# Silu in one ScalarE operation, a different VectorE order at the second phase of the way down, and the last two pairs of the last tile in two pieces

## The chip, the core and the metric

The kernel runs on one core of one Trainium2 chip. The metric is the time of one execution on the device in microseconds (us), as the median of several runs. Engines: TensorE (PE) multiplies matrices, VectorE (DVE) and ScalarE (ACT) work on tiles, GpSimd (POOL) does small things here, SyncE (SP) issues all large transfers.

## The reference

One layer of an encoder block on x of 512 tokens by 1024 channels, all in float32, then a final RMSNorm. The change touches the second half of the layer, a SwiGLU:

```
h = rms_norm(x, ffn_norm)                      # 512 x 1024
a, b = split(h @ w_gate_up, 2)                 # w_gate_up 1024 x 5632, a and b 512 x 2816
x = x + (silu(a) * b) @ w_down                 # silu(a) = a * sigmoid(a); w_down 2816 x 1024
return rms_norm(x, final_norm)
```

The first half (RMSNorm, one input projection of 6664 columns, forgetting attention, pooling, short convolution, gates, output projection) is the same in both kernels.

## The kernel before

**Arithmetic.** Every float32 product is made of three matmuls on split operands. A weight tile w is cast by ScalarE into a high part (`whi`), VectorE subtracts it from w to get the low part (`wlo`), and TensorE adds high*high, high*low and low*high. So every weight tile goes over SyncE (load into `raw`), ScalarE (`split_hi`, `parts_hi`, which raise `w_hi`), VectorE (`split_lo`, L1283; `parts_lo`, L1598, which raise `w_lo`) and TensorE. `raw`, `whi` and `wlo` are rings; SyncE's next load into a slot waits for `w_lo` of the unit that held it.

**Gate and up** (stages `ffn_first`, `ffn`, `ffn_last`). For each of 22 blocks of 128 hidden units TensorE makes two banks of 128x512, the gate and the up half. VectorE scales each by the row's 1/rms (`gate_rows`, L1625, `up_rows`, L1630), ScalarE computes the sigmoid of the gate into `SG`, and VectorE multiplies gate by sigmoid (L1617) and that by up (L1619). Two blocks form a pair; for a pair VectorE then makes the differences and sums that the way down uses (`hid_sum`), and splits them (`hid_low`).

**The way down** (product with `w_down`) is one level of a Strassen-like scheme with 7 products instead of 8, over R = 11 pairs, in four phases of TensorE. Phase 1 makes two products for every pair, 12 matmuls of 128x512 a pair, into banks `AB` and `DB_`. Phase 2 makes three, 18 matmuls a pair, into `FB_`, `DB_` and `AB`. Phase 3 makes one into `EB`, phase 4 one onto `FB_`. The weights of a product are blocks of `w_down` or sums of them, which VectorE also makes (`first_sum`, L1607; `second_sums`, L1716 and L1717; `third_sum`). Nothing plans this order at run time: it is written out by hand, one queue for each engine, and all waits are on semaphores. An engine that waits holds up all that stands behind it in its queue.

**Where phase 1 passes to phase 2.** TensorE's first pair of phase 2 (r = 0) takes in turn `FB_` (needs `w_lo` of the first two parts), `AB` (needs the third part, and `added` of 1 and 2: VectorE has added what the two `AB` banks held to the output x2), and `DB_` (needs `added` of 3 and 4). The next pair (r = 1) begins with `FB_` and the first two parts of its weights. VectorE's order for r = 0 is: two parts of pair 0 (one instruction, L1598), `second_sums(1)` (two), the third part of pair 0, `added` 1 and 2, `added` 3 and 4 (four instructions of L1741), `second_lo(8)` (L1681, the low part of hidden sums that TensorE needs for pair 8). Then r = 1 begins with two parts of pair 1.

**The end.** In phase 4 TensorE finishes `FB_[0]` for all pairs, then adds pairs 5 to 9 into `FB_[1]`, and puts the last pair (r = 10) of the last tile of tokens into two other banks in two pieces of 256 columns. VectorE adds `FB_[1]` to x2 (L1879), then each piece (`x2_piece`, L1833), scales tile 2 for output (`right_out(2)`, L1853), adds up the squares of the first piece that ScalarE made (L1888), makes those of the second piece (L1891) and the variance (L1840). GpSimd raises it to -0.5 (L577), ScalarE (`left_out`, L1244) and VectorE (`right_out`) scale the last tile, and SyncE writes it (L519), in the order left, right of tile 2, then left, right of each piece. ScalarE squares the first piece (L1237) and scales the left half of tile 2 after it.

Of the kernel before, what the change touches and what calls it, by code (L numbers as in the profile page):

```python
# [64 lines left out]

    "vector_step": dict(norm=19, front=23, pair=13, mix=2, ffn_first=7, ffn=15, ffn_last=8,
                        down=4),
# [34 lines left out]
def hybrid_block(nc, x, attn_norm, w_in, b_forget, b_gate, w_proj_attn, pool_w, pool_scale,  # L102
# [26 lines left out]
    with ExitStack() as ctx:  # L129
# [153 lines left out]
        def wk(slot, n=S, rows=slice(0, P)):  # L283
            return work[rows, slot * S:slot * S + n]
# [28 lines left out]
        ROWS4 = [(r,) for r in range(4)] + [(r, r + 1) for r in range(4, R - 1, 2)] + [(R - 1,)]  # L313
        LATE = 5
        ROWS3 = [(0,)] + [(r, r + 1) for r in range(1, R, 2)]
# [269 lines left out]
        def _(pe):  # L585
# [312 lines left out]
            mm.then_inc(full[FB_[0]], 1)  # L898
            for r in range(LATE, R - 1):
                mm = times(FB_[1], hid(r, A22 - 2), hid(r, A22), U_4 + r, 1, False, r == R - 2, True)  # L900
            mm.then_inc(full[FB_[1]], 1)
            pe.wait_ge(added, 14)
            for piece, b in zip(PIECES[TB - 1], LAST_BANKS):
                times(b, hid(R - 1, A22 - 2), hid(R - 1, A22), U_4 + R - 1, 1, True, True,
                      piece=piece).then_inc(full[b], 1)

# [4 lines left out]
        def _(act):  # L911
# [226 lines left out]
            def hidden(stage, i, j):  # L1138

                wait_free(act, (2 * j + 2) % 6, stage, i, j // 3 + 1)  # L1140
                tile(wk(SG), wk(A1), ACT.Sigmoid)
                split_hi(stage, i, 2 * j + 3)
                if stage != "ffn_first" and j % 2 == 0:
                    r = i * 3 + j // 2 if stage == "ffn" else R - 2 + j // 2
                    act.wait_ge(hid_sums, r + 1)
                    nc.scalar.copy(hid(r, S1_ + 2, 2), hid_32(r, S1_, 2)).then_inc(hid_hi, 1)  # L1146
                split_hi(stage, i, 2 * j + 4)
# [5 lines left out]
            tile(stat[:, 12:16], stat[:, 8:12], ACT.Exp, scale=-0.5)  # L1153
            nc.scalar.preload_act_table(ACT.Sigmoid)
            wait_full(act, 6, "ffn_first", 0, 1)
# [7 lines left out]
            wait_free(act, 0, "ffn_first", 0, 1)  # L1163
            tile(wk(SG), wk(A1), ACT.Sigmoid)
            split_hi("ffn_first", 0, 3)
# [5 lines left out]
            wait_free(act, 4, "ffn_last", 0, 1)  # L1171
            tile(wk(SG), wk(A1), ACT.Sigmoid)
            split_hi("ffn_last", 0, 5)
            second_hi(0)
            down_hi(0)
            wait_free(act, 0, "ffn_last", 0, 1)
            tile(wk(SG), wk(A1), ACT.Sigmoid)
            second_hi(1)
# [82 lines left out]
        def _(dve):  # L1261
# [348 lines left out]
            def gate_times_up(stage, i, j, r, odd):  # L1610

                a = (2 * j + 2) % 6 if stage != "ffn_first" else 0
                k = j // 3 + 1
                wait_free(dve, a, stage, i, k)
                dve.wait_ge(scalar_tile, count("scalar_tile", stage, i,
                                               j + 1 if stage != "ffn_first" else 3))
                step(nc.vector.tensor_tensor(wk(HD_), wk(A1), wk(SG), ALU.mult))  # L1617
                wait_free(dve, a + 1, stage, i, k)
                step(nc.vector.tensor_tensor(hid_32(r, A12 if odd else A11, 2), wk(HD_), wk(B1),  # L1619
                                             ALU.mult))  # L1620
# [144 lines left out]
            for r in range(R):  # L1765
                u, s = U_2 + 3 * r, (R + r) % SLOTS
                parts_lo(u, raw[:, s, 0:2 * HALF], 2)
                if r + 1 < R:
                    second_sums(r + 1)
                parts_lo(u + 2, chain(r))  # L1770
                if r == 0:
                    for m in range(2):
                        bank_done(AB[m], 1, U_2 - 2)
                        add_bank(AB[m], m, 1, ALU.add)
                    for m in range(2):
                        bank_done(DB_[m], 1, U_2 - 1)
                        add_bank(DB_[m], 2 + m, 0, ALU.subtract)
                if r < 3:
                    second_lo(R - 3 + r)
                if r >= 3:  # L1780
                    third_lo(r - 3)

            third_low(0)
            third_lo(R - 3)
            third_sum(0)
# [80 lines left out]
            for t in range(2):  # L1866
# [12 lines left out]
            step(nc.vector.tensor_tensor(tok(big_x, t, 1), banks[FB_[1]][:], tok(big_x, t, 1),  # L1879
                                         ALU.add))  # L1880
            x2_piece(t, 0)
            x2_piece(t, 1)
            right_out(2)
            lo, hi = PIECES[t][1]
            x2 = tok(big_x, t, 1)[:, lo:hi]
            dve.wait_ge(x2_square, t + 1)
            part = stat[:, SS_SUM:SS_SUM + 1]
            step(nc.vector.scalar_tensor_tensor(out=part, in0=square_sum(t), scalar=1.0 / D,  # L1888
                                                in1=left_part(t), op0=ALU.mult, op1=ALU.add))
            dve.wait_ge(x2_done, TB + 1)  # L1890
            step(nc.vector.scalar_tensor_tensor(  # L1891
                out=wk(HD_, hi - lo), in0=x2, scalar=1.0, in1=x2, op0=ALU.mult,
                op1=ALU.mult, accum_out=square_sum(TB)))
            variance(t, square_sum(TB), part)
# [28 lines left out]
```

## Time and profile before

| | |
|---|---|
| runs (us) | 806.82, 808.43, 2974.62; median 808.43 |
| profiled execution (us) | 808.46 |
| its span, first to last instruction (us) | 806.4 |
| TensorE busy | 787.4 us, 98% |
| VectorE busy | 505.2 us, 63% |
| ScalarE busy | 324.0 us, 40% |
| GpSimd busy | 21.0 us, 3% |
| granted TensorE clock, mean | 0.997 |

In the rows below a start is in us from the start of the span, the number behind it is the length in us, and brackets give the engine's idle time before the instruction and what ended it. Matmuls overlap, so the distance of their starts counts, not their length. The same holds for VectorE: an instruction of 0.69 us that waits for nothing lets the next one start after about 0.60 us.

### The profile page before, as it was taken

What the parts mean: (1) busy time and instruction counts of PE and PEld (TensorE: products, weight loads), DVE (VectorE), ACT (ScalarE), POOL (GpSimd) and SP (SyncE); (2) the same over time, 40 slices, a digit from 0 to 9 for tenths busy, and PEclk for the clock granted to TensorE, in tenths of its full rate; (3) what the DMA queues carried; (4) which work ended last, traced back from release to release, by engine and by line L of the source; (5) the groups of instructions that cost most, each with busy time, mean ns of one, the idle gap of its engine ahead of it and who ended that gap; (6) DMA issues with size and microseconds to landing.
All of it is one profiled execution on the core that took longest, in us unless ns stands there. A gap on an engine that the chain in (4) does not pass through costs nothing.

```text
span 806.4 us, 10953 instructions
## 1 busy us (share of the span) xinstructions
PE 787.4 (98%) x3568; PEld 652.7 (81%) x3568; DVE 505.2 (63%) x763; ACT 324.0 (40%) x520; POOL 21.0 (3%) x43
## 2 busy tenths in 40 slices
PE   5999999999999999999999999999999999999996
PEld 4878888888888888888888888888888888877885
DVE  7878686868634333443333465555555556799996
ACT  7265555555422222232223532222222222565554
POOL 4011010100000000000000000000000000000001
PEclk9999999999999999999999999999999999999998
DMA  7423232323243333334233233333333332353522
GB/s 223 124 78 92 56 100 55 101 54 102 56 110 96 104 104 97 85 91 117 81 102 99 59 105 94 89 104 104 104 92 90 104 104 88 123 170 118 164 85 104
DMA packets 128670, 81.18 MB, mean 101 GB/s; under 512 B 5420, under 2 KB 118116, under 8 KB 128644
## 3 DMA queue, kind: packets, MB, share of 16 engines
q1 hardware_dynamic: 128132, 80.79, 34.1%
q8 instruction: 14, 0.23, 0.1%
q0 software_dynamic: 512, 0.07, 0.1%
q14 instruction: 12, 0.10, 0.0%
HBM read 78.67 MB, written 2.10 MB: 100 GB/s over the span
## 4 chain that ended last, share of the span: by engine, by line
PE 92%; DVE 5%; DMA 1%; issue 1%; ACT 0%; SPq 0%; POOLq 0%; POOL 0%; ACTq 0%; DVEq 0%
PE bank L600 24%; PE bank L604 24%; PE bank L602 24%; PE bank L859 3%; PE bank L861 3%; PE bank L860 3%; PE bank L781 2%; PE bank L777 2%; PE bank L779 2%; PE bank L714 1%; DVE wlo L1598 1%; PE bank L631 1%; DVE operands L1681 1%; PE bank L694 1%; PE bank L739 1%
## 5 line engine op out<-in xcount | busy, mean ns | idle before, releaser
L600 PE MATMUL bank<-operands,whi 128*128 128x512 f32 x864 | 338.1, 391 | 1.0 <-DVE operands L1292 1.0
L604 PE MATMUL bank<-operands,wlo 128*128 128x512 f32 x864 | 336.4, 389 | 0.0
L602 PE MATMUL bank<-operands,whi 128*128 128x512 f32 x864 | 336.2, 389 | 0.0
L1283 DVE TENSOR_TENSOR wlo<-raw,whi 128x1024 fp32r<-128x1024 f32 x116 | 142.0, 1225 | 140.2 <-ACT whi L918 137.4
L600 PEld LDWEIGHTS bank<-operands,whi 128*128 128x128 f32 x864 | 162.2, 188 | 34.7 <-issue 1.4
L604 PEld LDWEIGHTS bank<-operands,wlo 128*128 128x128 f32 x864 | 162.2, 188 | 34.3
L602 PEld LDWEIGHTS bank<-operands,whi 128*128 128x128 f32 x864 | 162.2, 188 | 33.4 <-issue 0.2
L918 ACT CAST whi<-raw 128x1024 fp32r<-128x1024 f32 x116 | 121.1, 1045 | 70.4 <-PE bank L604 47.9
L924 ACT ACTIVATE work<-work 128x512 f32<-128x512 f32 (+1 forms) x24 | 15.2, 632 | 82.9 <-DVE work L1625 80.8
L1065 ACT ACTIVATE work<-bank,vecs 128x512 f32<-128x512 f32 x24 | 16.6, 690 | 78.0 <-PE bank L604 78.0
L1522 DVE TENSOR_TENSOR work<-bank,work 128x512 f32<-128x512 f32 x24 | 15.8, 688 | 41.1 <-PE bank L604 29.6
L861 PE MATMUL bank<-whi,operands 128*128 128x512 f32 x96 | 37.4, 390 | 0.0
L921 ACT ACTIVATE operands<-work 128x512 f32 (+2 forms) x24 | 15.2, 632 | 54.5 <-DVE work L1539 27.5
L859 PE MATMUL bank<-whi,operands 128*128 128x512 f32 x90 | 35.3, 392 | 0.0
L860 PE MATMUL bank<-wlo,operands 128*128 128x512 f32 x90 | 35.0, 389 | 0.0
L1146 ACT CAST operands<-tiles (+1 forms) x10 | 6.2, 622 | 62.4 <-DVE tiles L1636 62.4
L1630 DVE TENSOR_TENSOR work<-bank,big_y 128x512 f32<-128x512 f32 x22 | 15.2, 691 | 24.1 <-PE bank L604 24.0
L1625 DVE TENSOR_TENSOR work<-bank,big_y 128x512 f32<-128x512 f32 x22 | 15.1, 688 | 22.6 <-PE bank L604 17.6
L1022 ACT ACTIVATE big_y<-big_y,stat 128x128 f32<-128x128 f32 (+3 forms) x32 | 17.6, 552 | 22.1 <-DVE stat L1454 21.6
L1290 DVE TENSOR_TENSOR operands<-work,operands 128x512 f32 (+2 forms) x24 | 16.6, 690 | 14.4 <-ACT operands L921 13.4
L777 PE MATMUL bank<-whi,operands 128*128 128x512 f32 x64 | 25.0, 390 | 0.0
L781 PE MATMUL bank<-whi,operands 128*128 128x512 f32 x64 | 24.9, 389 | 0.0
(213 smaller groups left out, 842.3 us busy)
## 6 DMA issues: line engine op xcount, KB each, us to landing
raw<-in_w_in_dram SPq DMA_DIRECT2D x106, 256.0 KB, 3.2
raw<-in_w_gate_up_dram SPq DMA_DIRECT2D x88, 256.0 KB, 3.1
raw<-in_w_down_dram SPq DMA_DIRECT2D x55, 256.0 KB, 2.9
raw<-in_w_out_dram SPq DMA_DIRECT2D x16, 256.0 KB, 3.0
big_x<-in_x_dram SPq DMA_DIRECT2D x4, 512.0 KB, 3.8
raw<-in_w_proj_attn_dram SPq DMA_DIRECT2D x8, 256.0 KB, 2.8
raw<-in_w_proj_pool_dram SPq DMA_DIRECT2D x8, 256.0 KB, 3.1
raw<-in_w_proj_conv_dram SPq DMA_DIRECT2D x8, 256.0 KB, 3.0
```

The source lines that it names most:

```text
L600: nc.tensor.matmul(banks[b][:, 0:width], whi[:, s, w], op(hi + k * S), start=a, stop=False)
L602: nc.tensor.matmul(banks[b][:, 0:width], whi[:, s, w], op(lo + k * S), start=False, stop=False)
L604: mm = nc.tensor.matmul(banks[b][:, 0:width], wlo[:, s, w], op(hi + k * S), start=False, stop=z)
L777: nc.tensor.matmul(to, op(hi + at, P), whi[:, s, w], start=a, stop=False)
L781: mm = nc.tensor.matmul(to, op(lo + at, P), whi[:, s, w], start=False, stop=z)
L859: nc.tensor.matmul(to, h, wh, start=first, stop=False, skip_group_check=onto)
L860: nc.tensor.matmul(to, h, wl, start=False, stop=False, skip_group_check=onto)
L861: return nc.tensor.matmul(to, l, wh, start=False, stop=last, skip_group_check=onto)
L918: nc.scalar.copy(whi[:, s, :], raw[:, s, :]).then_inc(w_hi, 1)
L1022: e = nc.scalar.activation(lg, lg, ACT.Exp, bias=stat[:, 16 + at:17 + at], accum_out=stat[:, 24 + at:25 + at])
L1065: nc.scalar.activation(wk(GA + br), banks[b][:], ACT.Sigmoid, bias=vecs[:, bass.ds(i * 2 + (V_GATE + br * DB + mm), 1)]).then_inc(free[b], 1)
L1283: nc.vector.tensor_tensor(wlo[:, s, :], raw[:, s, :], whi[:, s, :].bitcast(F32), ALU.subtract).then_inc(w_lo, 1)
```

## The change

The sigmoid becomes `Silu` with the table preloaded for it, and VectorE's L1617 goes, so that the product with up (L1619) reads `SG` directly; its wait for the gate bank goes too, the one for the up bank stays. In phase 2 `second_sums(1)` moves behind `added` 1 and 2 and ahead of `added` 3 and 4, each `second_lo` moves from r to r+1 (first from r = 0 to r = 1), and each `third_lo` by one as well, so that one of them comes after the first part of phase 3. In phase 4 pairs 9 and 10 both go in two pieces of 256 columns, so that `FB_[1]` is full one pair earlier. VectorE scales tile 2 for output before it adds the pieces, and makes the second piece's squares before it takes in those of the first. No transfer is added or removed, and SyncE's and GpSimd's code is the same.

```diff
--- before.py
+++ after.py
@@ -63,7 +63,7 @@
     "row_max": dict(pair=2), "exp_done": dict(pair=2), "probs": dict(pair=2),
     "v_lo_part": dict(pair=2),
 
-    "vector_step": dict(norm=19, front=23, pair=13, mix=2, ffn_first=7, ffn=15, ffn_last=8,
+    "vector_step": dict(norm=19, front=23, pair=13, mix=2, ffn_first=6, ffn=9, ffn_last=5,
                         down=4),
 }
 
@@ -311,7 +311,7 @@
         AB, DB_, FB_, EB = (2, 3), (6, 7), (4, 5), (0, 1)
         N1 = 0
         ROWS4 = [(r,) for r in range(4)] + [(r, r + 1) for r in range(4, R - 1, 2)] + [(R - 1,)]
-        LATE = 5
+        LATE, LAST = 5, R - 2
         ROWS3 = [(0,)] + [(r, r + 1) for r in range(1, R, 2)]
 
 
@@ -896,13 +896,16 @@
                 pe.wait_ge(w_lo, U_4 + r + 1)
                 mm = times(FB_[0], hid(r, A22 - 2), hid(r, A22), U_4 + r, 0, False, r == R - 1, True)
             mm.then_inc(full[FB_[0]], 1)
-            for r in range(LATE, R - 1):
-                mm = times(FB_[1], hid(r, A22 - 2), hid(r, A22), U_4 + r, 1, False, r == R - 2, True)
+            for r in range(LATE, LAST):
+                mm = times(FB_[1], hid(r, A22 - 2), hid(r, A22), U_4 + r, 1, False, r == LAST - 1,
+                           True)
             mm.then_inc(full[FB_[1]], 1)
             pe.wait_ge(added, 14)
             for piece, b in zip(PIECES[TB - 1], LAST_BANKS):
-                times(b, hid(R - 1, A22 - 2), hid(R - 1, A22), U_4 + R - 1, 1, True, True,
-                      piece=piece).then_inc(full[b], 1)
+                for r in range(LAST, R):
+                    mm = times(b, hid(r, A22 - 2), hid(r, A22), U_4 + r, 1, r == LAST, r == R - 1,
+                               piece=piece)
+                mm.then_inc(full[b], 1)
 
 
 
@@ -1138,7 +1141,7 @@
             def hidden(stage, i, j):
 
                 wait_free(act, (2 * j + 2) % 6, stage, i, j // 3 + 1)
-                tile(wk(SG), wk(A1), ACT.Sigmoid)
+                tile(wk(SG), wk(A1), ACT.Silu)
                 split_hi(stage, i, 2 * j + 3)
                 if stage != "ffn_first" and j % 2 == 0:
                     r = i * 3 + j // 2 if stage == "ffn" else R - 2 + j // 2
@@ -1151,7 +1154,7 @@
             tile(stat[:, 8:12], stat[:, 4:8], ACT.Ln)
             act.wait_ge(scalar_tile, count("scalar_tile", "ffn_first", 0, 1))
             tile(stat[:, 12:16], stat[:, 8:12], ACT.Exp, scale=-0.5)
-            nc.scalar.preload_act_table(ACT.Sigmoid)
+            nc.scalar.preload_act_table(ACT.Silu)
             wait_full(act, 6, "ffn_first", 0, 1)
             nc.scalar.copy(RSTD, banks[6][:]).then_inc(free[6], 1)
             def second_hi(r):
@@ -1161,7 +1164,7 @@
                 nc.scalar.copy(high2(r, S4_, 3), hid_32(r, S4_, 3)).then_inc(hid2_hi, 1)
 
             wait_free(act, 0, "ffn_first", 0, 1)
-            tile(wk(SG), wk(A1), ACT.Sigmoid)
+            tile(wk(SG), wk(A1), ACT.Silu)
             split_hi("ffn_first", 0, 3)
             split_hi("ffn_first", 0, 4)
             with act.Fori(0, 3) as i:
@@ -1169,12 +1172,12 @@
                     hidden("ffn", i, j)
             hidden("ffn_last", 0, 0)
             wait_free(act, 4, "ffn_last", 0, 1)
-            tile(wk(SG), wk(A1), ACT.Sigmoid)
+            tile(wk(SG), wk(A1), ACT.Silu)
             split_hi("ffn_last", 0, 5)
             second_hi(0)
             down_hi(0)
             wait_free(act, 0, "ffn_last", 0, 1)
-            tile(wk(SG), wk(A1), ACT.Sigmoid)
+            tile(wk(SG), wk(A1), ACT.Silu)
             second_hi(1)
             down_hi(1)
             act.wait_ge(hid_sums, R)
@@ -1611,12 +1614,10 @@
 
                 a = (2 * j + 2) % 6 if stage != "ffn_first" else 0
                 k = j // 3 + 1
-                wait_free(dve, a, stage, i, k)
                 dve.wait_ge(scalar_tile, count("scalar_tile", stage, i,
                                                j + 1 if stage != "ffn_first" else 3))
-                step(nc.vector.tensor_tensor(wk(HD_), wk(A1), wk(SG), ALU.mult))
                 wait_free(dve, a + 1, stage, i, k)
-                step(nc.vector.tensor_tensor(hid_32(r, A12 if odd else A11, 2), wk(HD_), wk(B1),
+                step(nc.vector.tensor_tensor(hid_32(r, A12 if odd else A11, 2), wk(SG), wk(B1),
                                              ALU.mult))
 
             def gate_rows(stage, i, j):
@@ -1765,22 +1766,24 @@
             for r in range(R):
                 u, s = U_2 + 3 * r, (R + r) % SLOTS
                 parts_lo(u, raw[:, s, 0:2 * HALF], 2)
-                if r + 1 < R:
+                if 1 <= r < R - 1:
                     second_sums(r + 1)
                 parts_lo(u + 2, chain(r))
                 if r == 0:
                     for m in range(2):
                         bank_done(AB[m], 1, U_2 - 2)
                         add_bank(AB[m], m, 1, ALU.add)
+                    second_sums(1)
                     for m in range(2):
                         bank_done(DB_[m], 1, U_2 - 1)
                         add_bank(DB_[m], 2 + m, 0, ALU.subtract)
-                if r < 3:
-                    second_lo(R - 3 + r)
-                if r >= 3:
-                    third_lo(r - 3)
+                if 1 <= r < 4:
+                    second_lo(R - 4 + r)
+                if r >= 4:
+                    third_lo(r - 4)
 
             third_low(0)
+            third_lo(R - 4)
             third_lo(R - 3)
             third_sum(0)
             third_low(1)
@@ -1878,19 +1881,19 @@
             dve.wait_ge(added, 14)
             step(nc.vector.tensor_tensor(tok(big_x, t, 1), banks[FB_[1]][:], tok(big_x, t, 1),
                                          ALU.add))
+            right_out(2)
             x2_piece(t, 0)
             x2_piece(t, 1)
-            right_out(2)
             lo, hi = PIECES[t][1]
             x2 = tok(big_x, t, 1)[:, lo:hi]
+            dve.wait_ge(x2_done, TB + 1)
+            step(nc.vector.scalar_tensor_tensor(
+                out=wk(HD_, hi - lo), in0=x2, scalar=1.0, in1=x2, op0=ALU.mult,
+                op1=ALU.mult, accum_out=square_sum(TB)))
             dve.wait_ge(x2_square, t + 1)
             part = stat[:, SS_SUM:SS_SUM + 1]
             step(nc.vector.scalar_tensor_tensor(out=part, in0=square_sum(t), scalar=1.0 / D,
                                                 in1=left_part(t), op0=ALU.mult, op1=ALU.add))
-            dve.wait_ge(x2_done, TB + 1)
-            step(nc.vector.scalar_tensor_tensor(
-                out=wk(HD_, hi - lo), in0=x2, scalar=1.0, in1=x2, op0=ALU.mult,
-                op1=ALU.mult, accum_out=square_sum(TB)))
             variance(t, square_sum(TB), part)
             right_out(t)
             leave()
```

## Rows read from the trace of the kernel before

**Rows 1.** Busy time of each engine in two stretches: us, instructions in brackets

```profile
400.00:600.00 200.00, 200.00 (x898) 165.69 (x897) 106.71 (x143) 62.28 (x87) 0.00 (x0) 1.00 0.32 95
...
720.00:740.00 20.00, 17.95 (x77) 13.97 (x77) 20.00 (x28) 9.93 (x15) 0.00 (x0) 1.00 0.38 125
```

**Rows 2.** The gate's multiplication, grouped by line, from 400 us to the end

```profile
L1617 DVE TENSOR_TENSOR work<-work 128x512 f32<-128x512 f32 x22 | 15.0, 683 | 0.0
```

**Rows 3.** VectorE in order of time, 691 to 727 us: start, length, idle before

```profile
691.19 0.69 DVE L1630 TENSOR_TENSOR work<-bank,big_y 128x512 f32<-128x512 f32 x1 [0.65 <-PE bank L604]
691.80 0.68 DVE L1617 TENSOR_TENSOR work<-work 128x512 f32<-128x512 f32 x1
692.52 0.69 DVE L1619 TENSOR_TENSOR last_tile<-work 128x512 f32<-128x512 f32 x1
...
704.66 0.69 DVE L1607 TENSOR_TENSOR early<-raw 128x512 f32<-128x512 f32 x1 [2.65 <-DMA raw<-in_w_down_dram]
...
720.72 1.22 DVE L1598 TENSOR_TENSOR wlo<-raw,whi 128x1024 fp32r<-128x1024 f32 x1
...
723.66 2.47 DVE L1741 TENSOR_TENSOR big_x<-big_x,bank 128x512 f32<-128x512 f32 x4
726.05 0.95 DVE L1681 TENSOR_TENSOR operands<-tiles,operands 128x768 fp32r<-128x768 f32 x1
726.92 1.22 DVE L1598 TENSOR_TENSOR operands<-raw,operands 128x1024 fp32r<-128x1024 f32 x1
```

**Rows 4.** TensorE in order of time: first matmuls of the way down, then the transition

```profile
690.99 0.39 PE L859 MATMUL bank<-whi,operands 128*128 128x512 f32 x1
...
722.03 0.47 PE L859 MATMUL bank<-whi,high 128*128 128x512 f32 x1 [0.41 <-issue]
...
724.48 0.47 PE L859 MATMUL bank<-operands,high 128*128 128x512 f32 x1 [0.82 <-DVE big_x L1741]
...
728.28 0.47 PE L859 MATMUL bank<-operands,high 128*128 128x512 f32 x1 [0.81 <-DVE operands L1598]
```

**Rows 5.** The seventh load of the way down: SyncE's issues, then time to landing

```profile
L487 SPq DMA_DIRECT2D raw<-in_w_down_dram x2: 327/863/1399, 699.6 to 700.0; - x2
...
DMA to landing us min/median/max: 3.0/3.8/4.7
```

**Rows 6.** ScalarE in order of time: casts before and after a table load

```profile
694.50 0.61 ACT L1128 CAST whi<-raw 128x512 fp32r<-128x512 f32 x1
695.02 0.61 ACT L1128 CAST whi<-flat 128x512 fp32r<-128x512 f32 x1
695.65 1.28 ACT L1190 ACT_TABLE_LOAD   x1
696.95 0.62 ACT L1128 CAST operands<-raw 128x512 fp32r<-128x512 f32 x1
```

**Rows 7.** All engines in order of time at the end, 797 to 802 us

```profile
797.41 0.55 POOL L577 TENSOR_TENSOR stat<-stat 128x1 f32<-128x1 f32 x1 [2.60 <-DVE stat L1840]
...
798.22 0.39 PE L861 MATMUL bank<-whi,operands 128*128 128x512 f32 x1
...
798.45 0.28 PE L859 MATMUL bank<-whi,last_tile 128*128 128x256 f32 x1
...
798.65 0.69 DVE L1879 TENSOR_TENSOR big_x<-bank,big_x 128x512 f32<-128x512 f32 x1 [1.31 <-PE bank L861]
...
799.37 0.76 DVE L1833 TENSOR_TENSOR big_x<-bank,big_x 128x256 f32<-128x256 f32 x2
...
800.04 0.74 DVE L1853 SCALAR_TENSOR_TENSOR tiles<-big_x,stat,work 128x512 f32<-128x512 f32 x1
...
800.70 0.15 DVE L1888 SCALAR_TENSOR_TENSOR stat<-stat 128x1 f32<-128x1 f32 x1
800.89 0.43 DVE L1891 SCALAR_TENSOR_TENSOR work<-big_x 128x256 f32<-128x256 f32 x1
...
801.60 0.55 POOL L577 TENSOR_TENSOR stat<-stat 128x1 f32<-128x1 f32 x1 [3.64 <-DVE stat L1840]
```

## The prediction

> **What bounds the kernel now.** I read the busy time by stretch first, for which engine is full where. In the long gate-and-up stage TensorE is busy for all of 200.00 us and VectorE for 106.71; in the 20 us around the passage to the second phase it is the other way round, VectorE 20.00 and TensorE 17.95 [rows 1]. So VectorE work taken away before that passage is worth nothing to the end, and in it each microsecond may count. Then VectorE and TensorE in order of time. From 728.28 us to the row at 798.22 TensorE issues 308 further matmuls of 512 columns (180 of phase 2's last ten pairs, 66 of phase 3, 63 of phase 4, less the first): 69.94 us, or 0.227 each, without a pause [rows 4, 7]. By that pace the way down's first matmul at 690.99, with 132 matmuls in phase 1 and 18 in pair 0 of phase 2 behind it, would reach pair 1 at 690.99 + 150 x 0.227 = 725.04 us. It does at 728.28. **3.24 us** are lost there, some in phase 1, the rest in the waits of [rows 4], and that is all that the passage can give back.
>
> Who holds it up is VectorE: pair 1 starts 1.36 us after VectorE starts on its weights (726.92 to 728.28), and VectorE works without a gap from 704.66 to there [rows 3, 4]. Its last idle time, 2.65 us before 704.66, ends with the seventh load of the way down [rows 3]. SyncE issued that load when VectorE had finished weights two operations earlier, so it too hangs on VectorE; one of its two issues took 1.40 us where the other took 0.33, and one half landed after 4.7 us, the other after 3.0 [rows 5]. The last stretch, after TensorE, is one chain: VectorE adds the pieces, squares, makes the variance, GpSimd takes the power at 801.60, and 4.8 us of scaling and writing follow to 806.4 [rows 7].
>
> **The change, part by part.**
>
> *Silu.* It removes 22 multiplications of 683 ns, 15.0 us of VectorE [rows 2]. 21 lie where TensorE has no pause, cover enough even if ScalarE's Silu took twice the sigmoid's time, so I count them as nothing. The last one stands at 691.80, ahead of the way down. It started 0.61 us after the scaling of the up half (691.19) and needed no wait for it; the next product started 0.72 later, at 692.52, after a wait [rows 3]. Without it that product has to wait for the scaling itself, to 691.19 + 0.72 = 691.91. The gain is 692.52 - 691.91 = **0.61 us**, not 0.72. Everything behind it up to the seventh load follows a chain of VectorE, ScalarE and SyncE without slack that I can find, so I take the load, and the start at 704.66, to move with it. Bounds: 0 if the landing time does not follow, and if the 1.40 us issue falls back to the other's 0.33, 1.07 more [rows 5]. I take 0.61 as VectorE's code changes and SyncE's does not. A Silu that cost ScalarE more would be late at nobody here: between its tile and 691.19 VectorE waits 0.65 us for TensorE [rows 3].
>
> *The order at the passage.* `second_lo(8)`, 726.05 to 726.92, was ahead of pair 1's weights and now is behind them: **0.87 us** [rows 3]. Nobody needs it before pair 8. With the two moves the weights of pair 1 start at 726.92 - 0.61 - 0.87 = 725.44 and TensorE's pair 1 at 725.44 + 1.36 = 726.80. The other half of this edit, `second_sums(1)` between the two pairs of additions, moves no work across pair 1; it makes the `AB` additions earlier and leaves the `DB_` additions last. Does one of them bind? Four additions take 2.39 (723.66 to 726.05), 0.60 each, so the first for `DB_` starts at 725.44 - 1.20 = 724.24. TensorE started 0.82 after such an addition did (723.66 to 724.48), so at 725.06 [rows 3, 4]. Six matmuls, 1.36, make it 726.42, before 726.80. They bind nothing but eat what the early `AB` wins. The pauses then are 0.47 ahead of pair 0 (its weights at 720.11, 1.31 later at 721.42, against 690.99 + 132 x 0.227 = 720.95), 0.92 ahead of `DB_` (721.42 + 12 x 0.227 = 724.14), 0.38 ahead of pair 1: 1.77 of the 3.24 remain. Late next is VectorE again. After that it needs for a pair the two-part operation (1.22 long, 1.13 to the next, as 0.69 gives 0.60), three short ones and a `second_lo`: 1.13 + 3 x 0.60 + 0.87 = 3.80 us [rows 3], against 18 x 0.227 = 4.09 of TensorE, so no new wait builds up. ScalarE's cast for pair 1 waits for the first of the moved sums: from 724.24 - 1.20 = 723.04 to 723.73. Two parts take about 2 x 0.52 = 1.04 (estimated from [rows 6]), so it is there at 724.8, 0.6 before 725.44. The moved low parts of phase 3 lie under TensorE's 4.09 us a pair: nothing. Passage: 0.61 + 0.87 = **1.48 us**. SyncE's loads of phase 2 wait for weights that come earlier or at the same place in the queue, so no load is put off.
>
> *The last two pairs in pieces.* Three matmuls of 512 columns become six of 256. The only rows of such pieces are the six from 798.45; the first three take the time to a pitch near 0.118 against half of 0.227, 0.03 us more in all [rows 7]. `FB_[1]` is full three matmuls earlier, so its addition goes from 798.65 to 797.97; VectorE was idle for 1.31 before it [rows 7]. The copy-out of tile 2 comes next, at 797.97 + 0.72 = 798.69 (GpSimd's power for it is done at 797.96), and takes 0.66 (800.04 to 800.70). So the pieces are added from 799.35, as before (799.37), and TensorE's last piece ends at about the old time, 799.35, before the second one needs it. Two additions take 0.67 (799.37 to 800.04) and the wait for the second about 0.1: the squares start at 800.12. From there to GpSimd was 0.71, and now the small sum of 0.19 (800.70 to 800.89) lies between [rows 7]: 800.12 + 0.71 + 0.19 = 801.02, say 801.05 with the 0.03. Gain: 801.60 - 801.05 = **0.55 us**. Nothing of the pieces themselves; the copy-out in the idle time makes it. Bounds: 0 if the writes behind it cannot start sooner, 0.66 if the whole copy-out goes.
>
> Sum, against the profiled execution: 808.46 - 1.48 - 0.55 = **806.4 us**. The median of the runs shown is 808.43, so the same holds for it.
>
> **Rivals.**
>
> *The landing does not follow.* The seventh load comes when it did; Silu gives nothing, and 808.46 - 0.87 - 0.55 = 807.0. For it: one issue of 1.40 us in [rows 5] that no operation of VectorE explains. Against: the load is issued by VectorE's progress.
>
> *The landing gets shorter.* The 1.40 us issue was an accident, and 1.07 us more come off: 805.4. The floor is 808.46 - 3.24 - 0.55 = 804.7.
>
> *The writes bind.* SyncE writes tile 2's left half first, which ScalarE makes no sooner than before, and the last four writes then share the way with it. The tail gives 0: 807.0.
>
> *Table loads, and slower than before.* If Silu's table did not serve the casts as well, ScalarE would change tables before every Silu and again behind it. A load put the next cast 1.93 us behind the last (695.02 to 696.95) where casts follow after 0.52 (694.50 to 695.02), so 1.41 a switch [rows 6]. In the gate-and-up stage that is hidden, as TensorE has no pause and ScalarE is busy for 62.28 of 200 us [rows 1]. At the last Silu, two switches put off weights that stand ahead of 691.19 in VectorE's queue by 2.82 us; 0.65 of idle time there absorbs a part [rows 3]. The total is 2 x 1.41 - 0.65 - 0.61 - 0.87 - 0.55 = +0.14: 808.6. It turns from gain to loss at 1.34 us a switch. Against it: the sigmoid lives with the same casts, and the load in [rows 6] stands where the code asks for one. The Trainium skill's page "ScalarE: Activation LUTs", section "What ACT_TABLE_LOAD costs", gives 1.28 us and a drain of 1.38, 2.66 us for a switch; at that price this rival would be 811.1, but the row shows the 1.28 and no such drain. The same page's section "Table sets: the hidden batching unit" says that cheap functions such as copy are in every set, which speaks against the rival; no row here has a Silu in it.
>
> *It does not do what it says.* Silu's last gain and the order's are both taken up by a wait that I don't see (ScalarE's cast for pair 1 is the closest): 808.46 - 0.55 = 807.9.
>
> **Numbers.** Forecast as summed 0.5; landing fixed 0.13; landing shorter 0.15; writes bind 0.08; a hidden wait 0.1; table loads 0.04. The range goes from the floor, 804.7, to 808.3, which takes in all but the last case and also that two runs of the kernel before differ by 1.6 us. Two per cent, about what a measurement of this kernel can tell from no change, is 16 us; no case comes near it: within 2% 0.98, 0.01 on either side.
>
> **What would show it.** Right: no multiplication at L1617 and as many table loads as before; the idle time before the way down's seventh load ends about 0.6 us earlier; `DB_` of pair 0 waits about 0.9 us, pair 1 starts about 1.5 us earlier against the way down's first matmul; the last power starts 2.0 us earlier than 801.60, and 4.8 us follow. Wrong: a pause of TensorE later than pair 1, a table load between Silu and a cast, VectorE waiting for ScalarE's cast at pair 1, or more than 5 us behind the last power.

## The result: 2.0 us faster, ratio 0.9975

| | before | changed |
|---|---|---|
| median of 13 runs each (us) | 807.39 | 804.84 |
| ratio, 95% interval | | 0.9975 [0.9967, 0.9983] |
| profiled execution, its span (us) | 808.46, 806.4 | 806.28, 804.3 |

The ratio is 2.0 us of 808 (1.4 to 2.7); the medians alone are 2.55 apart. The one run of 2974.62 us among those before is left out of the ratio. Forecast were 806.4 against 808.46, so 2.03 us, and the range of 804.7 to 808.3 holds the 804.84 near its lower end. A second comparison in another series gave 0.9974 [0.9964, 0.9985]. The intervals are about 0.1% wide to each side, much finer than the two per cent of the forecast.

The two spans differ by 2.1 us, but they can't be set side by side as they are. From TensorE's first product of a weight tile on, the marks below compare them. The way down's first matmul came 1.45 us later in the changed kernel, because the transfers at the start took longer (the four of x took 4.5 us to land in the median, 3.8 before); the 675.0 us between are equal.

| mark (us) | before | changed | difference |
|---|---|---|---|
| first product of a weight tile | 15.96 | 17.38 | +1.42 |
| from there to the way down's first matmul | 675.03 | 675.06 | +0.03 |
| from there to pair 1 of phase 2 | 37.29 | 34.30 | -2.99 |
| from there to the last power on GpSimd | 73.32 | 72.72 | -0.60 |
| from there to the end | 4.8 | 4.8 | 0.0 |

The profile after, busy time of the engines in the stretches of [rows 1]:

```profile
400.00:600.00 200.00, 200.00 (x899) 165.70 (x898) 99.61 (x131) 62.61 (x86) 0.00 (x0) 1.00 0.32 94
...
720.00:740.00 20.00, 19.90 (x89) 16.08 (x88) 20.00 (x29) 10.55 (x15) 0.00 (x0) 1.00 0.41 132
```

VectorE has 7 us less to do in the long stage and no other engine is faster for it. In the passage VectorE is still full, but TensorE's pause has shrunk from 2.05 to 0.10 us.

All lines with a table load, from the groups by line (count, then busy us and mean ns), and the 22 gate functions, from the groups by line and shape behind 400 us:

```profile
L930 ACT ACT_TABLE_LOAD x1 | 1.3, 1283 | 0.7 <-PEq L1914 0.7
L1058 ACT ACT_TABLE_LOAD x1 | 1.3, 1283 | 0.0
L1152 ACT ACT_TABLE_LOAD x1 | 1.3, 1283 | 0.0
L1157 ACT ACT_TABLE_LOAD x1 | 1.3, 1283 | 0.0
L1193 ACT ACT_TABLE_LOAD x1 | 1.3, 1283 | 0.0
```

```profile
L927 ACT ACTIVATE work<-work 128x512 f32<-128x512 f32 x22 | 13.9, 632 | 80.2 <-DVE work L1626 80.2
```

Five loads, each where the code asks for one, as before; a Silu takes 632 ns, as the sigmoid did. The rival with table loads is dead. The Trainium skill's page "ScalarE: Activation LUTs", section "Table sets: the hidden batching unit", says that copy is in every set, and the trace agrees.

VectorE in order of time, the instructions that answer to [rows 3], and TensorE's that answer to [rows 4]:

```profile
692.64 0.69 DVE L1631 TENSOR_TENSOR work<-bank,big_y 128x512 f32<-128x512 f32 x1 [0.65 <-PE bank L604]
693.44 0.69 DVE L1620 TENSOR_TENSOR last_tile<-work 128x512 f32<-128x512 f32 x1
...
703.80 0.69 DVE L1610 TENSOR_TENSOR early<-raw 128x512 f32<-128x512 f32 x1 [0.98 <-DMA raw<-in_w_down_dram]
...
724.18 1.28 DVE L1742 TENSOR_TENSOR big_x<-big_x,bank 128x512 f32<-128x512 f32 x2
725.38 1.22 DVE L1601 TENSOR_TENSOR operands<-raw,operands 128x1024 fp32r<-128x1024 f32 x1
```

```profile
692.44 0.39 PE L859 MATMUL bank<-whi,operands 128*128 128x512 f32 x1
...
725.09 0.39 PE L859 MATMUL bank<-whi,high 128*128 128x512 f32 x1
...
726.74 0.47 PE L859 MATMUL bank<-operands,high 128*128 128x512 f32 x1
```

Against the way down's first matmul (690.99 before, 692.44 here) the sum on the seventh load moved from +13.67 to +11.36, by 2.31 us and not by 0.61. `DB_` starts at +32.65, its own pace (144 x 0.227 = 32.69), without the wait of 0.92 that was forecast. Pair 1 is at +34.30, 0.25 from that pace. The seventh load's issues and landings, to compare with [rows 5]:

```profile
L487 SPq DMA_DIRECT2D raw<-in_w_down_dram x2: 327/377/427, 700.5 to 700.9; - x2
...
DMA to landing us min/median/max: 2.5/2.7/2.9
```

No issue of 1.40 us and no landing of 4.7. This is the rival "the landing gets shorter": the gain ahead of pair 1 came out at 2.99 instead of 1.48. It was priced at 1.07 us, from the issues alone; the later half landed 1.8 us sooner after its issue began (2.9 against 4.7). And the end, to compare with [rows 7]:

```profile
796.18 0.28 PE L859 MATMUL bank<-whi,operands 128*128 128x256 f32 x1
...
796.38 0.69 DVE L1882 TENSOR_TENSOR big_x<-bank,big_x 128x512 f32<-128x512 f32 x1 [0.64 <-PE bank L861]
...
797.11 0.75 DVE L1856 SCALAR_TENSOR_TENSOR tiles<-big_x,stat,work 128x512 f32<-128x512 f32 x1
...
797.78 0.75 DVE L1836 TENSOR_TENSOR big_x<-bank,big_x 128x256 f32<-128x256 f32 x2
...
798.56 0.42 DVE L1890 SCALAR_TENSOR_TENSOR work<-big_x 128x256 f32<-128x256 f32 x1
...
799.03 0.16 DVE L1895 SCALAR_TENSOR_TENSOR stat<-stat 128x1 f32<-128x1 f32 x1
...
799.46 0.55 POOL L577 TENSOR_TENSOR stat<-stat 128x1 f32<-128x1 f32 x1 [3.09 <-DVE stat L1843]
```

VectorE's idle time ahead of the full bank fell from 1.31 to 0.64, the copy-out stands in what is now free, and the squares start 0.78 after the first piece's addition, where 1.52 were (799.37 to 800.89).

### The profile page after: what moved, and what is told of

Read it like the earlier page. It is cut to its first block, busy times and chain, and to the rows that moved or that the text cites. A ratio compares the mean times of both kernels' runs of the same rounds, so it can differ in the third digit from the quotient of the medians.

```text
span 804.3 us, 10900 instructions
## 1 busy us (share of the span) xinstructions
PE 786.6 (98%) x3571; PEld 653.7 (81%) x3571; DVE 491.9 (61%) x741; ACT 324.2 (40%) x520; POOL 20.5 (3%) x43
## 4 chain that ended last, share of the span: by engine, by line
PE 96%; DVE 1%; issue 1%; DMA 1%; ACT 0%; POOLq 0%; POOL 0%; ACTq 0%; SPq 0%; DVEq 0%
PE bank L600 24%; PE bank L602 24%; PE bank L604 24%; PE bank L859 4%; PE bank L861 4%; PE bank L860 4%; PE bank L777 2%; PE bank L779 2%; PE bank L781 2%; PE bank L714 1%; PE bank L694 1%; PE bank L739 1%; PE bank L692 1%; PE bank L737 1%; DMA big_x<-in_x_dram 1%
## 5 line engine op out<-in xcount | busy, mean ns | idle before, releaser
L1068 ACT ACTIVATE work<-bank,vecs 128x512 f32<-128x512 f32 x24 | 16.5, 689 | 78.0 <-PE bank L604 78.0
L1525 DVE TENSOR_TENSOR work<-bank,work 128x512 f32<-128x512 f32 x24 | 15.8, 688 | 41.2 <-PE bank L604 29.6
L861 PE MATMUL bank<-whi,operands 128*128 128x512 f32 (+1 forms) x97 | 37.5, 387 | 0.0
L860 PE MATMUL bank<-wlo,operands 128*128 128x512 f32 (+1 forms) x91 | 35.2, 387 | 0.0
L859 PE MATMUL bank<-whi,operands 128*128 128x512 f32 (+1 forms) x91 | 35.2, 387 | 0.0
L1293 DVE TENSOR_TENSOR operands<-work,operands 128x512 f32 (+2 forms) x24 | 16.5, 689 | 14.4 <-ACT operands L924 13.4
L777 PE MATMUL bank<-whi,operands 128*128 128x512 f32 x64 | 25.0, 390 | 0.0
L781 PE MATMUL bank<-whi,operands 128*128 128x512 f32 x64 | 24.9, 389 | 0.0
```

Of the source, the lines that this page charges most:

```text
L777: nc.tensor.matmul(to, op(hi + at, P), whi[:, s, w], start=a, stop=False)
L781: mm = nc.tensor.matmul(to, op(lo + at, P), whi[:, s, w], start=False, stop=z)
L859: nc.tensor.matmul(to, h, wh, start=first, stop=False, skip_group_check=onto)
L860: nc.tensor.matmul(to, h, wl, start=False, stop=False, skip_group_check=onto)
L861: return nc.tensor.matmul(to, l, wh, start=False, stop=last, skip_group_check=onto)
L1068: nc.scalar.activation(wk(GA + br), banks[b][:], ACT.Sigmoid, bias=vecs[:, bass.ds(i * 2 + (V_GATE + br * DB + mm), 1)]).then_inc(free[b], 1)
```

## The experiments

Open after this: why the landing differs, whether each part is worth what the sum says, and which part of the tail makes it. Twelve further kernels ran (two of them without an edit), each timed in five rounds and profiled once. All marks are in us: "seventh load" is VectorE's first sum on it and "pair 1" the first matmul of pair 1 in phase 2, both from the way down's first matmul; "tail" goes from pair 1 to the last power. "Behind" is the power to the end. The interval of a ratio is about 0.0009 wide to each side, 0.7 us, and the ratios of the three parts alone (e2, e3, e4) can't be told from 1. That can't size a part, so the marks do; each comes from one profiled execution of its kernel. Code cuts leave out the counts of VectorE's steps, which change with the edit.

| | seventh load | pair 1 | tail | behind | ratio |
|---|---|---|---|---|---|
| before, as first profiled | 13.67 | 37.29 | 73.32 | 4.8 | |
| changed, as first profiled | 11.36 | 34.30 | 72.72 | 4.8 | 0.9975 |
| e1 before again | 12.16 | 35.78 | 73.32 | 4.8 | 1.0010 |
| e2 Silu only | 11.36 | 35.08 | 73.30 | 4.8 | 0.9998 |
| e3 order only | 11.86 | 34.66 | 73.30 | 4.8 | 1.0001 |
| e4 tail only | 12.68 | 36.30 | 72.76 | 4.8 | 1.0000 |
| e5 changed again | 11.36 | 34.80 | 72.76 | 4.8 | 0.9974 |
| e6 product back in 21 blocks | 11.37 | 34.15 | 72.74 | 4.8 | 0.9975 |
| e7 product back in the last | 11.87 | 34.63 | 72.73 | 4.8 | 0.9977 |
| e8 pieces, VectorE as before | 11.43 | 34.31 | 72.98 | 4.8 | 0.9973 |
| e9 VectorE's tail, no pieces | 11.34 | 35.04 | 73.44 | 4.8 | 0.9986 |
| e10 before, low part moved | 12.01 | 37.29 | 73.30 | 4.8 | 1.0007 |
| e11 changed, low part moved | 11.70 | 35.65 | 72.71 | 4.8 | 0.9985 |
| e12 and small sum on ScalarE | 13.10 | 35.15 | 72.71 | 5.0 | 0.9987 |

**e1, the kernel before once more.** No edit.

> The kernel before, once more, against itself. Ratio 1.000 within 0.001. Marks, measured from the first matmul of the way down in each profile: VectorE's first sum on the seventh load at +13.67 us in the first profile, +11.36 with the change; first matmul of pair 1 of phase 2 at +37.29 and +34.30. Theory 1 (the 1.40 us issue of the seventh load and its late landing were an accident of one execution): this run shows issues of 0.33 to 0.43 us, the seventh load at about +12.0 (11.36 + 0.61) and pair 1 at about +35.8. Theory 2 (it belongs to the kernel before and its timing, and Silu took it away): again an issue over 1 us, +13.7 and +37.3.

The same code, 1.5 us earlier at the seventh load, and 23.62 us from there to pair 1 both times. The sum on the seventh load in e1, and its two issues:

```profile
703.17 0.69 DVE L1607 TENSOR_TENSOR early<-raw 128x512 f32<-128x512 f32 x1 [1.24 <-DMA raw<-in_w_down_dram]
```

```profile
L487 SPq DMA_DIRECT2D raw<-in_w_down_dram x2: 328/376/425, 699.6 to 700.0; - x2
...
DMA to landing us min/median/max: 2.5/2.9/3.2
```

Theory 1 holds: the late landing was luck of the execution, not of the code. Even so e1's sum is 0.3 us later than in e3, which has the same code up to there: both issue the load at the same mark, and its later half took 3.2 us to land in e1 and 2.9 in e3. The traces show one thing that differs between the two executions of the kernel before. In each of the 14 there is one transfer of 16 KB, of the kind that the profile calls "instruction", between +8 and +17 of the way down. The row of it in the kernel before from 699.3 to 699.6 us, at +8.5, and in e1 from 707.1 to 707.4, at +16.3 (queue, packets, MB, share):

```profile
q8 instruction: 1, 0.02, 30.1%
```

```profile
q8 instruction: 1, 0.02, 20.8%
```

At +8.5 it falls on the seventh load's issue, in the kernel before and in e4, and those two have late sums, 13.67 and 12.68. The third late one, 13.10 in e12, has it at +10.6, while half of that load was on its way. In the changed kernel it came at +15.5, beside the tenth load, where VectorE waited only 0.09 us. That the transfer causes the late landing is an inference from its place in these traces; no run moved it on purpose. The ratio of 1.0010 [1.0001, 1.0019] for equal code tells how far a ratio here is to be trusted: e2 to e4, taken in the same series, are 0.0012, 0.0009 and 0.0010 below it, 0.7 to 1.0 us each, with intervals as wide as that.

**e2, Silu only**, and **e7, the product put back in the last block** of the changed kernel (its result is not used; cut from the edit):

```diff
+                if stage == "ffn_last" and j == 2:
+                    step(nc.vector.tensor_tensor(wk(HD_), wk(A1), wk(SG), ALU.mult))
```

> Silu alone; order and tail as before. Theory 1: seventh load at +11.4 where its landing is normal, pair 1 0.61 us earlier than in the run of the kernel before of this job (if that one is at +35.8, here +35.2), time 0.6 us less, ratio 0.9992. Theory 2: landing 2.3 us earlier than the kernel before, pair 1 at +35.0 against +37.3, time 2.3 us less, ratio 0.997. Rival with table loads: more than 5 ACT_TABLE_LOAD in the trace and a ratio over 1.

> The changed kernel with that multiplication put back in the last block alone, 0.68 us of VectorE. Prediction's step: the seventh load and pair 1 of phase 2 come 0.61 us later than in the changed kernel with the same landing: VectorE's first sum on the seventh load at +12.0 (+11.4 without), but pair 1 at most 0.4 us later where TensorE had reached its own pace. Rival: no shift, the gain was the landing alone.

Where the landing is undisturbed the sum on the seventh load stands at 11.34 to 11.43 with Silu (the changed kernel, e2, e5, e6, e8, e9) and at 11.86 and 11.87 without its effect in the last block (e3, e7). So the last product is worth **0.50 us** there. SyncE's issue shows it free of the landing: the seventh load's starts at +8.06 or +8.07 in all eight executions with Silu's effect in the last block, and at +8.59 in all six without it, 0.53 us later. So the load follows VectorE, as the forecast assumed. The two issues in the changed kernel and in e7, whose first matmuls of the way down start at 692.44 and 690.77:

```profile
700.50 0.80 SPq L487 DMA_DIRECT2D raw<-in_w_down_dram  x2
```

```profile
699.36 0.80 SPq L487 DMA_DIRECT2D raw<-in_w_down_dram  x2
```

The scaling and the products in e7:

```profile
690.97 0.69 DVE L1633 TENSOR_TENSOR work<-bank,big_y 128x512 f32<-128x512 f32 x1 [0.64 <-PE bank L604]
691.57 0.68 DVE L1620 TENSOR_TENSOR work<-work 128x512 f32<-128x512 f32 x1
692.29 0.69 DVE L1622 TENSOR_TENSOR last_tile<-work 128x512 f32<-128x512 f32 x1
```

1.32 us from the scaling to the product with up. Without the middle one it is 0.80 (692.64 to 693.44 in the changed kernel), not the 0.72 of the forecast, and from the 1.33 between the two in the kernel before (691.19 to 692.52) that leaves the gain of 0.53. Why it is 0.80 is not shown. That the scaling reads a bank does not explain it: in an earlier stage of the changed kernel a sum that waits for a product which reads a bank starts 0.73 after it (406.25 to 406.98, L1525 to L1542). The product with up waits for ScalarE's `SG` as well, in the code.

**e6, the product put back in the other 21 blocks** (same lines with `not`).

> The changed kernel with the multiplication of gate and gate function put back on VectorE in the first 21 of 22 blocks (its result is not used). 14.3 us of VectorE more. Prediction's step: worth nothing, all marks and the time as in the changed kernel within 0.1 us, ratio as e5. Rival (VectorE's load counts in the long stage): TensorE's 675.0 us from its first weight product to the way down grow, or the ratio goes back towards 1.

14.3 us more of VectorE and nothing moved later: 675.02 us to the way down, seventh load at 11.37, pair 1 at 34.15. The part costed at nothing is worth nothing.

**e3, the order only.**

> The new order at the passage alone. Both theories: pair 1 0.87 us earlier than the kernel before with the same landing, and nothing before the passage changes: with a normal landing +34.9 (theory 1), with the late one +36.4 (theory 2). From pair 1 to the last power 73.3 us as before. Ratio 0.9989. If the additions into the DB banks bind, a wait of TensorE for VectorE's L1741 of about 0.9 us ahead of the DB matmuls.

From the seventh load to pair 1 it is 22.80 us instead of 23.62: **0.82** of the 0.87 forecast, with Silu away. The landing was a little sooner than the one of e1, so pair 1 came at 34.66.

**e4, the tail only; e8, pieces with VectorE's old order; e9, VectorE's new order without the pieces.** e8 takes the change's hunk on TensorE alone, e9 the one on VectorE's end alone, both with Silu and the order at the passage.

> Pieces of the last two pairs and VectorE's new order at the end alone. From pair 1 to the last power 72.7 us instead of 73.3, 4.8 us behind it, pair 1 where the kernel before has it. Ratio 0.9993. If the writes bind: 5.4 us behind the power and a ratio of 1.000.

> The changed kernel with TensorE's pieces, but VectorE's order at the end as before (the pieces added ahead of the copy-out of tile 2, the small sum ahead of the squares). The prediction said that the copy-out in the idle time makes the gain and the pieces alone nothing. By the same rows: addition of the full bank at -0.68, pieces as soon as they are there, the second at about -0.3, then the copy-out of 0.66 as before: from pair 1 to the last power 73.0 (73.3 before, 72.7 changed). If the pieces alone made it: 72.7. If nothing: 73.3.

> The changed kernel with VectorE's new order at the end, but TensorE's pieces as before (only the last pair in two pieces). Theory (idle time made by the earlier full bank is what the copy-out fills): the bank is full 0.68 us later, the copy-out then delays the pieces, squares at 800.83 in the clock of the first profile, small sum 0.19 behind them: from pair 1 to the last power 73.45, later than the 73.3 of the kernel before. If the order helps by itself as it did on top of the pieces (0.24): 73.1.

The pieces alone take 0.34 off the tail, VectorE's order alone adds 0.12, both take off 0.58. VectorE in e8, with the old order and more pieces:

```profile
795.40 0.69 DVE L1882 TENSOR_TENSOR big_x<-bank,big_x 128x512 f32<-128x512 f32 x1 [0.64 <-PE bank L861]
796.18 0.42 DVE L1836 TENSOR_TENSOR big_x<-bank,big_x 128x256 f32<-128x256 f32 x1
796.83 0.42 DVE L1836 TENSOR_TENSOR big_x<-bank,big_x 128x256 f32<-128x256 f32 x1 [0.22 <-PE bank L861]
797.17 0.74 DVE L1856 SCALAR_TENSOR_TENSOR tiles<-big_x,stat,work 128x512 f32<-128x512 f32 x1
```

The second piece waits 0.22 us for TensorE, and the copy-out stands behind it; with the new order it fills that gap and VectorE's wait for the first piece. In e9 nothing is full earlier, so the copy-out puts the pieces off. The timed ratios don't tell e8 (0.9973) from the changed kernel (0.9974 in the same series), so the 0.24 us of VectorE's order stand on the marks alone. That e9 has pair 1 at 35.04 is no part of its edit: half of its eighth load landed after 4.7 us, with the 16 KB transfer at +12.4 meanwhile, and VectorE waited 0.85.

**e5, the changed kernel once more.**

> The changed kernel once more. In the profiles so far the parts add up in the trace (0.6 for Silu, 0.8 for the order, 0.6 for the tail, 2.0 us in all), but alone none stood out of the noise of the timed runs (0.9998, 1.0001, 1.0000, and 1.0010 for the kernel before against itself). Theory 1 (sum, with landing and start as luck): pair 1 at +34.2 to +34.8, from there to the last power 72.7, ratio 0.9975. Rival (the parts cancel in the timed runs and the first measurement was luck of the day): same marks, ratio 0.999 or above.

The sum holds, and so does the luck: e5 waits for the tenth load once more, 0.59 us, and has pair 1 at 34.80 instead of 34.15 to 34.31. One issue of that load took 1.43 us there, with the 16 KB transfer at +15.6.

**e10, e11: `second_lo(2)` into VectorE's idle time ahead of the seventh load**, on the kernel before and on the changed one.

```diff
                 parts_lo(NU + 2 * r, raw[:, s, 0:HALF])
+                if r == 5:
+                    second_lo(r - 3)
                 if r + 1 < R:
                     first_sum(r + 1)
...
                 parts_lo(NU + 2 * r + 1, chain(r))
-                if r >= 5:
+                if r > 5:
                     second_lo(r - 3)
```

> The kernel before with one step moved: second_lo(2), 0.87 us of VectorE, goes ahead of the first sum on the seventh load, into VectorE's idle time there. No work is taken away. Theory (pair 1 is set by all of VectorE's work behind the seventh load's landing): pair 1 0.6 us earlier than at a landing as in the second run of the kernel before (+35.8 there), 0.87 at a late one: +34.9 to +35.2 where the landing is the usual one, ratio 0.999. Rival (what counts is only what Silu and the order took away): +35.8 to +37.3.

> The changed kernel with the same move. Pair 1 of phase 2 is then at TensorE's own pace, +34.0 to +34.1, in every execution, also where a load lands up to 0.8 us late; the changed kernel has had +34.15 to +34.80. Ratio 0.9970. If moving it makes the weights of the sixth pair late: a wait of TensorE in phase 1 and pair 1 above +34.3.

What was expected of both fell, and in each the rival or the "if" came: pair 1 came 1.5 us later than in e1 and 0.8 to 1.5 later than in e5, e6 and e8. The idle time at the seventh load is filled, and another one opens at the ninth. VectorE in e11:

```profile
701.86 0.96 DVE L1682 TENSOR_TENSOR operands<-tiles,operands 128x768 fp32r<-128x768 f32 x1 [0.22 <-ACT operands L1164]
702.74 0.69 DVE L1610 TENSOR_TENSOR early<-raw 128x512 f32<-128x512 f32 x1
703.34 0.68 DVE L1601 TENSOR_TENSOR wlo<-early,whi 128x512 fp32r<-128x512 f32 x1
...
709.28 0.69 DVE L1610 TENSOR_TENSOR early<-raw 128x512 f32<-128x512 f32 x1 [1.75 <-DMA raw<-in_w_down_dram]
```

The slot of the ninth load comes free with the subtraction at 703.34, which the moved step puts off: its issue is at +13.08, against +12.75 in the changed kernel, while VectorE reaches the sum sooner. But that delay of 0.33 is not the loss. One of its halves then took 4.8 us to land (5.2 in e10), and the 16 KB transfer of these two executions, at +15.7 in e11 and +16.5 in e10, fell while it was on its way. Had that half landed after the usual 2.9 us, it would have been there at +16.3 in e11, before VectorE came to the sum at +16.5 (an estimate from these marks). So in the traces the late landing is the whole loss. The timed ratios (0.9985 and 1.0007) say that there is no gain, and e11's eleven runs lie within 0.9 us of each other, so the loss is hardly luck of one execution. Whether the move brings the late landing about stays open.

**e12, e11 with the small sum of the last tile on ScalarE.**

```diff
+            act.wait_ge(x2_square, 4)
+            nc.scalar.activation(stat[:, SS_SUM:SS_SUM + 1], stat[:, SS_LAST + 3:SS_LAST + 4],
+                                 ACT.Identity, bias=stat[:, 19:20], scale=1.0 / D
+                                 ).then_inc(x2_square, 1)
             left_out(2)
...
```

> The kernel of the run before this one, and the small sum between the squares and the variance of the last tile made by ScalarE behind its own squares instead of by VectorE. It stood 0.19 us on the last chain. From pair 1 to the last power 72.53 to 72.6 instead of 72.7; ScalarE's left half of tile 2 about 0.25 us later, with 4.8 us behind the power as before. If the later write of that half binds, the 4.8 grow by 0.2. Ratio 0.9968.

No gain: the tail is 72.71 as in e11. ScalarE's sum and VectorE's variance in e12:

```profile
798.17 0.29 ACT L1258 ACTIVATE stat<-stat 128x1 f32<-128x1 f32 x1
...
798.58 0.16 DVE L1849 SCALAR_TENSOR_TENSOR stat<-stat 128x1 f32<-128x1 f32 x1 [0.18 <-ACT stat L1258]
```

A tile of one column costs ScalarE 0.29 us, and VectorE now waits 0.18 for it, what it saved. The left half of tile 2 goes out later and 0.2 us more follow the power. No version ran ahead of the changed kernel by more than the noise.

## Why the prediction was right

- **VectorE sets the passage, and its work in the long stage is worth nothing: right** (e6; the windows after).
- **Silu, 0.61 forecast, 0.53 measured at the load's issue, 0.50 at VectorE's sum.** The step that was off is the wait of the product for the scaling, 0.80 instead of 0.72.
- **The order, 0.87 forecast, 0.82 measured** (e3).
- **No wait for `DB_` of more than was won: right in kind.** The 0.92 was computed for a late seventh load. With a usual landing VectorE is earlier by more than that, and the wait was gone in the changed kernel, e6 and e8. Where a load came late behind the new order (e5, e9, e11, e12), TensorE lost 0.4 to 0.8 us ahead of `DB_`.
- **The tail, 0.55 forecast, 0.56 to 0.60 measured, but for a reason that was half wrong.** "Nothing of the pieces themselves; the copy-out in the idle time makes it" does not hold: the pieces alone give 0.34, because with VectorE's old order too the additions and the squares stand earlier; the copy-out needs them and adds 0.24. The sum was made with both at once and never for the pieces alone.
- **The landing.** The forecast gave 0.15 to a shorter one and priced it at 1.07 us. In the profiled pair it came so, and took 1.70 us, and e1 shows it to be luck. So three of the signs named did not show in that pair as forecast: the seventh load came 2.31 us earlier and not 0.6, `DB_` did not wait 0.9, and pair 1 came 2.99 earlier and not 1.5. Against e1 pair 1 came 1.48 earlier, but 0.3 of that is e1's own landing.
- **The time.** With undisturbed landings the marks give 0.50 + 0.82 + 0.58 = 1.90 us, and the ratio says 2.0, no finer than 1.4 to 2.7. That the late landing is as frequent in the timed runs of both kernels, so that the ratio does not hold it, is not shown: of the five profiled executions without Silu two had it at the seventh load, of the nine with Silu one.
- **Luck in the absolute number.** The profiled 806.28 lies beside the forecast's 806.4 because the start was 1.42 us later and the gain ahead of pair 1 1.51 larger than forecast, and the two cancel. And 806.4 was counted down from 808.46, while eight of the twelve runs of the kernel before, besides the one of 2974.62, lie from 806.53 to 807.48. So the median of 804.84 came in 1.6 us below it. A forecast for one profile alone could have missed by as much as most of the change is worth.

## What to carry over

A change of 2 us in 800 is read from marks in the trace that start where the change does, not from the span: the start alone moved by 1.4 us between two profiles, and one late transfer by 1.5 in equal code. Filling an idle time of the bounding engine is worth something only if the next load is there when the engine comes to it sooner: in e10 and e11 the idle time went to another load and nothing was won. Two edits of one tail must be summed apart and together, as one can make the room that the other uses.

## What the runs showed of the hardware

- One 16 KB transfer of the kind "instruction" fell within the first 17 us of the way down in every execution, at +8.5 in two, +10.6 and +12.4 in one each, +15.4 to +16.5 in ten, and for equal code at +8.5 and +16.3. In 11 of the 14 one of SyncE's issues beside it took 0.60 to 1.48 us instead of 0.33 to 0.43; in the other three (e10 to e12) none did, but half of a load landed after 4.6 to 5.2 us, where most took 2.5 to 3.3. The Trainium skill's page "Runtime: NRT & Kernel Launch", section "Instruction fetch mechanics", has code streamed in blocks of 16 KiB and calls the cost "mostly hidden". The size agrees; that it is hidden does not fit these traces, if the transfer is what holds the loads up, which no run tested.
- An instruction of VectorE without a wait started 0.60 us after the one before it (all 128x512, float32). One that waits for that one's result started 0.72 after it in the last block of the kernel before, where the operand lies in no bank, and 0.73 in an earlier stage, where the one before it reads a bank. From the scaling of the up half to the product with up it was 0.79 to 0.87 in the changed kernel's 22 blocks. What makes this one longer is not shown.
